# The gate projection in four pieces inside the first steps of the grid attention, and the decays by one fp32r product per head with their subtraction on ScalarE

## The reference, cut to what matters

```python
def hybrid_layer(x, ctx, ...):                      # x, ctx: 256 tokens each
    h  = modulate(rms_norm_2(x, norm1_w), sh1, sc1)
    hc = modulate(rms_norm_2(ctx, norm1_w), sh1c, sc1c)
    p  = h @ w_in                                   # q, k, v (512 each), z (512), xs, B, C, dt
    attn = neighbourhood_attention(q, k, v, kc, vc, rpb, rows)
    xs, bm, cm, dt = ssd_prep(...)                  # depthwise conv, silu, softplus
    y_ssd = ssd_bidirectional(z, xs, bm, cm, dt, a, ssd_d, ssd_norm_w, h_fwd, h_bwd)
    x = x + g1 * (concatenate([attn, y_ssd]) @ w_out)
    x = x + g2 * conv_glu(...)

def neighbourhood_attention(...):                   # per head: 256 grid keys and 256 context keys
    scores = concatenate([s_loc * scale + bias, s_ctx * scale])
    p = softmax(scores)                             # then p_loc @ v_win + p_ctx @ v_ctx

def ssd_chunked(xs, dt, a, bm, cm, h0):             # per direction
    cum = cumsum(dt * a)
    decay = exp(where(lower, cum[:, None] - cum[None, :], -inf))
    m = einsum("ign,jgn->ijg", cc, bc) * decay * dtc
    y_diag = einsum("ijge,jgep->igep", m, xc)
    y_off  = einsum(..., cc, h_in, exp(cum))

def ssd_bidirectional(z, ...):
    y = y_f + flip(y_b) + d_skip[:, None] * xs
    y = y.reshape(bsz, l, SSD_WIDTH) * silu(z)
    return rms_norm_2(y, norm_w)
```

## Time and profile before

| | |
|---|---|
| median of three executions | 1012.58 us |
| the profiled execution | 1013.08 us, its span 1011.2 us |
| TensorE busy | 978.2 us, 97% of the span |
| VectorE, ScalarE, GpSimd busy | 696.0, 511.3, 55.2 us |
| granted TensorE clock | 0.999 on the mean, the higher of its two levels (2.4 GHz) |
| grid stage, first S to first product of `w_out` | 718.7 to 783.3 us of the span |
| in it: TensorE, VectorE, ScalarE busy | 60.43, 53.49, 30.20 of 64.60 us |

### The profile page before, as it was taken

One profiled execution on the slowest core, in us unless ns is written; L12 is line 12 of the kernel. 1 busy time (PEld: TensorE's weight loads), 2 busy tenths in 40 slices (PEclk: granted clock), 3 DMA queues, 4 the chain that ended last, 5 costly groups with the idle time before them and its releaser, 6 DMA issues. The chain is left out here.

```text
span 1011.2 us, 14855 instructions
## 1 busy us (share of the span) xinstructions
PE 978.2 (97%) x5836; PEld 836.7 (83%) x5836; DVE 696.0 (69%) x997; ACT 511.3 (51%) x686; POOL 55.2 (5%) x73
## 2 busy tenths in 40 slices
PE   7989999999999999999999999999998989999997
PEld 4568899988978877899998987888865779999996
DVE  2576658999755665657778565456688587777775
ACT  2465565445446655544445563554444354444443
POOL 0210000000001200000001010000010000000000
PEclk9999999999999999999999999999999999999999
DMA  9122566767756633668887552234101336555541
GB/s 364 61 98 98 216 255 219 280 227 270 260 189 213 225 118 120 225 242 329 297 326 290 197 220 94 92 130 144 42 1 42 130 141 213 183 181 184 183 178 42
DMA packets 28943, 185.05 MB, mean 183 GB/s; under 512 B 3680, under 2 KB 4384, under 8 KB 9312
## 3 DMA queue, kind: packets, MB, share of 16 engines
q1 hardware_dynamic: 23472, 155.54, 42.6%
q0 software_dynamic: 4416, 28.31, 7.5%
q10 hardware_dynamic: 1008, 0.55, 0.2%
HBM read 181.76 MB, written 2.62 MB: 182 GB/s over the span
## 5 line engine op out<-in xcount | busy, mean ns | idle before, releaser
L1950 DVE TENSOR_TENSOR split<-raw,split 128x2048 fp32r<-128x2048 f32 x122 | 279.6, 2292 | 179.7 <-ACT split L1414 178.2
L1414 ACT ACTIVATE split<-raw 128x2048 fp32r<-128x2048 f32 x121 | 231.4, 1912 | 242.1 <-PE bank L710 224.9
L708 PE MATMUL bank<-acts,split 128*128 128x256 f32 (+1 forms) x960 | 278.5, 290 | 2.5 <-DVE acts L1990 1.4
L710 PE MATMUL bank<-acts,split 128*128 128x256 f32 (+1 forms) x960 | 276.7, 288 | 0.0
L709 PE MATMUL bank<-acts,split 128*128 128x256 f32 (+1 forms) x960 | 276.7, 288 | 0.0
L708 PE MATMUL bank<-split,acts 128*128 128x512 f32 (+1 forms) x544 | 211.1, 388 | 1.4 <-DVE split L1950 1.0
L709 PE MATMUL bank<-split,acts 128*128 128x512 f32 (+1 forms) x544 | 208.7, 384 | 0.0
L710 PE MATMUL bank<-split,acts 128*128 128x512 f32 (+1 forms) x544 | 208.6, 383 | 0.0
L708 PEld LDWEIGHTS bank<-acts,split 128*128 128x128 f32 x960 | 183.8, 191 | 10.0 <-issue 3.4
L709 PEld LDWEIGHTS bank<-acts,split 128*128 128x128 f32 x960 | 183.8, 191 | 3.6 <-issue 0.2
L710 PEld LDWEIGHTS bank<-acts,split 128*128 128x128 f32 x960 | 183.8, 191 | 1.9
(11 more groups left out here) (254 smaller groups left out, 1062.5 us busy)
## 6 DMA issues: line engine op xcount, KB each, us to landing
raw<-w_mlp SPq DMA_DIRECT2D x64, 1024.0 KB, 4.8
raw<-w_glu SPq DMA_DIRECT2D x22, 1024.0 KB, 4.8
bias<-w_ada POOLq DMA_DIRECT2D x14, 1024.0 KB, 6.7
raw<-w_qkv SPq DMA_DIRECT2D x12, 1024.0 KB, 5.1
arena<-w_glu_down SPq DMA_DIRECT2D x22, 512.0 KB, 3.3
work<-w_ada POOLq DMA_DIRECT2D x10, 1024.0 KB, 5.9
raw<-w_mla_o SPq DMA_DIRECT2D x4, 1024.0 KB, 5.1
raw<-w_moba_o SPq DMA_DIRECT2D x4, 1024.0 KB, 4.8
```

The costliest lines, as they stand in the source:

```text
L708: pe.matmul(out_, a[0], b[0], start=first, stop=False)
L710: return pe.matmul(out_, a[1], b[0], start=False, stop=last)
L1414: return act.activation(out_, in_, ACT.Copy)
L1950: v.tensor_tensor(split[:, c % 2, 1, 0:n], raw[:, c % 2, 0:n], split[:, c % 2, 0, 0:n].bitcast(F32), ALU.subtract).then_inc(lo_ready, 1)
```

## The change

1. The weights and products of z move behind those of k. z's 48 products are cut into four pieces of 12 (kind Z) that stand in steps 0 to 3 of the grid stage. ScalarE copies the two z units out of their banks at turns 3 and 5, and takes one Silu of both after the loop. VectorE multiplies by it after both y are summed.
2. The cumulative decays of the two directions lie on eight rows instead of sixteen, as a high part (rows 0 to 7) and a low part (rows 32 to 39), both fp32r. G is then one fp32r product of 128 x 512 with a column that has a one in either row.
3. The subtraction and the minimum of the decays leave VectorE: ScalarE computes relu(column - row) in four instructions right after it has copied the probabilities of turn i - 1, and then exp(-that), still in turn i. G h stands at the end of the step before that turn.
4. K goes into a small unit, which moves all small units behind it by one place, and it and the context keys' unit (C) stand ahead of P 0. `DECAY`, the places of F, Y and O, and the pair, segment and y banks are set anew.

```diff
-DECAY = (1, 2, 4, 5, 7, 8, 10, 11)
-SEGMENTS = [("G", 0), ("G", 1), ("K", 1), ("F", 0), ("G", 2), ("G", 3), ("F", 1), ("G", 4), ("G", 5), ("F", 2), ("G", 6),
-            ("G", 7), ("F", 3)]
-SEGMENT_STEP = {("K", 1): 1, **{("G", h): DECAY[h] - 2 for h in range(1, H)}, **{("F", n): 3 * n + 1 for n in range(4)}}
+DECAY = (0, 1, 5, 6, 8, 9, 11, 12)
+CARRIED = (3, 4, 8, 11)
...
+SEGMENT_STEP = {**{("G", h): DECAY[h] - 1 for h in range(1, H)}, **{("F", n): CARRIED[n] - 2 for n in range(4)}}
+MIXED = (4, 5, 7, 8, 10, 11, 13, 14)
+WEIGHTED = (3, 4, 6, 8, 10, 12, 14)
...
-    first = [("S", 0), ("S", 1), ("G", 0), ("S", 2)]
+    first = [("S", 0), ("S", 1), ("G", 0), ("S", 2), ("C", 1), ("K", 1)]
...
         steps.append(("P", i))
-        steps.extend(x for x in SEGMENTS if SEGMENT_STEP.get(x) == i)
         if i + 3 < 2 * H:
             steps.append(("S", i + 3))
-        if i - 1 in DECAY:
-            steps.append(("Y", DECAY.index(i - 1)))
-        if i % 2 == 0 and i:
-            steps.append(("O", i // 2 - 1))
+        if i < 4:
+            steps.append(("Z", i))
+        if i in MIXED:
+            steps.append(("Y", MIXED.index(i)))
+        if i in WEIGHTED:
+            steps.append(("O", WEIGHTED.index(i)))
+        steps.extend(x for x in SEGMENTS if SEGMENT_STEP.get(x) == i)
...
-            for name in ("v", "xs", "bc", "q", "z", "k"):
+            for name in ("v", "xs", "bc", "q", "k", "z"):
                 load_all(name)
...
-            rows_units(GC["z"], GU["z"], 4, 512, 512, both[:2], 2)
...
                 elif kind == "G":
                     segment_start(kind, i)
-                    for d in range(2):
-                        ins = pe.matmul(seg_bank[:, d * T:(d + 1) * T], repeated(ident, 8 * d + i, P),
-                                        cum_rows[:, d * T:(d + 1) * T], start=True, stop=True)
-                    ins.then_inc(seg_ready, 1)
+                    if i == 0:
+                        pe.wait_ge(cum_parts, 1)
+                    pe.matmul(seg_bank[:, :], repeated(pick[:, :], i, P), cumr[:, :], start=True, stop=True)\
+                        .then_inc(seg_ready, 1)
...
# ScalarE, turn i of its loop
-                if i - 1 in DECAY:
-                    h = DECAY.index(i - 1)
-                    act.wait_ge(seg_free, SEGMENTS.index(("G", h)) + 1)
-                    act.activation(E[h % 2], E[h % 2], ACT.Exp).then_inc(seg_exp, 1)
                 if i == 1:
                     context_keys(1)
+                    pair_empty(window_unit("K", 1), pair(nkT, 1))
+                    used(GC["k"] + 1)
+                if i == 3:
+                    gate_rows_out(0)
...
+                if i in DECAY:
+                    h = DECAY.index(i)
+                    segment_out(act, "G", h)
...
+                        ins = act.activation(E[h % 2][:, a:e], seg_bank[:, src:src + e - a], ACT.Relu, scale=-1.0,
+                                             bias=stat[:, c:c + 1])
+                    ins.then_inc(seg_free, 1)
+                    act.wait_ge(seg_free, SEGMENTS.index(("G", h)) + 1)
+                    act.activation(E[h % 2], E[h % 2], ACT.Exp, scale=-1.0).then_inc(seg_exp, 1)
                 if i in (6, 10):
                     pair_out(i // 4 - 1)
-                if i == 12:
-                    used(GC["k"] + 1)
+                if i in (4, 6):
+                    used(GC["z"] + i // 2 - 2)
+            for t in range(2):
+                gemm_gone(act, GU["z"] + t)
+            act.activation(sz, sz, ACT.Silu).then_inc(z_act, 1)
             pair_out(3)
...
# VectorE, after the cumulative decays, and turn i of its loop
+            step(v.tensor_tensor(pick[:, :], ident[:, 0:8], ident[:, 32:40], ALU.add))
+            step(v.tensor_copy(cumr[0:8, :], cum[0:8]))
+            settle()
+            v.tensor_tensor(cumr[32:40, :], cum[0:8], cumr[0:8, :].bitcast(F32), ALU.subtract).then_inc(cum_parts, 1)
...
-                if i in DECAY:
-                    decay(DECAY.index(i))
                 if i - 1 in DECAY:
                     matrix(DECAY.index(i - 1))
-                if i == 13:
+                if i == 1:
                     used(GC["k"] + 1)
-                if i == 14:
+                if i in (5, 7):
+                    used(GC["z"] + i // 2 - 2)
+                if i == 15:
                     gated_rows(0)
                 if i == 16:
                     gated_rows(1)
```

More of the change, by code:

```diff
@@ L204, in grid_order @@
     for kind, i in first + steps + [("T", 0), ("T", 1)]:
-        if kind in ("S", "P", "T"):
+        if kind in ("S", "P", "T", "K"):
             units[(kind, i)] = n
@@ L1164, in cumulative @@
                 b = sbank(u)
[L1165 to L1168, removed]
+                pe.matmul(b[0:8, 0:T], dA(0)[:, 0:8], const("upto"), start=True, stop=False)
+                pe.matmul(b[0:8, P:T], dA(1)[:, 0:8], const("upto", 0, P), start=False, stop=True)
+                pe.matmul(b[0:8, T:2 * T], dA(1)[:, 8:16], const("since"), start=True, stop=False)
+                pe.matmul(b[0:8, T:T + P], dA(0)[:, 8:16], const("since", P, P), start=False, stop=True)\
+                    .then_inc(small_ready, 1)
             def cumulative_columns():
@@ L1244, in segment_start, with gate_products @@
                 else:
-                    gemm_gone(pe, ku + 2)
+                    gemm_gone(pe, ku + 4)
+            def gate_products(t, part_):
+                u = GU["z"] + t
+                if t == 0:
+                    weights_in(GC["z"] + part_)
+                if part_ == 0:
+                    gemm_start(u)
+                w = slot(GC["z"] + part_, 4, 512)
+                for k in range(4):
+                    ins = product(gbank(u)[:, :], both[t](4 * part_ + k), tuple(p[:, k, :] for p in w),
+                                  part_ == 0 and k == 0, part_ == 1 and k == 3)
+                if part_:
+                    ins.then_inc(gemm_ready, 1)
+                elif t:
+                    ins.then_inc(down_used, 1)
             def grid_work(kind, i):
@@ L1773, in _ @@
                 small_empty(SU["xsrow"] + n, dst)
-            used(GC["z"])
-            used(GC["z"] + 1)
-            for t in range(2):
-                u = GU["z"] + t
-                gemm_out(act, u)
-                act.activation(sz[:, t, :], gbank(u)[:, :], ACT.Silu).then_inc(gemm_free[u % 4], 1)
             small_empty(SU["brow"], Bcr[:, :, :, :].rearrange("p a b c -> p (a b c)"))
@@ L2676, in gated_rows @@
                 v.tensor_tensor(yrow[:, t, :], y_banks[t][:, :], yrow[:, t, :], ALU.add).then_inc(y_free, 1)
-                v.wait_ge(y_free, t + 1)
-                step(v.tensor_tensor(yrow[:, t, :], yrow[:, t, :], sz[:, t, :], ALU.mult))
             def rows_means():
+                v.wait_ge(y_free, 2)
+                v.wait_ge(z_act, 1)
+                for t in range(2):
+                    step(v.tensor_tensor(yrow[:, t, :], yrow[:, t, :], sz[:, t, :], ALU.mult))
                 settle()
```

97 lines of the change are left out of this document (46 added, 51 removed).

## The result

The changed kernel takes 1037.97 us (median of 4 runs, 1036.30 to 1039.83), the kernel before 1012.62 in the same comparison: ratio 1.0252, 95% interval 1.0235 to 1.0268. The forecast was 1028.1 us with a range of 1019.5 to 1033.5. The direction was right, the size was not: 10 us are missing, and the time lies 4.5 us above the range. The profiled execution took 1037.91 us with a span of 1036.1 and a mean granted clock of 0.984, where before it was 0.999.

The account below looks back on a forecast made before the run. TensorE was taken to bound the grid stage, with ScalarE's late exponential making it wait: -8.6 gains + 23.7 new waits + 0.4 end = +15.5 us on the profiled 1013.08, giving a median of 1028.1 us, range 1019.5 to 1033.5.

Parts of the forecast that it names:

- The new wait: Grid stage, after each late G: S waits for ScalarE's tile exponential, 2.78 us for five heads; all new waits 23.7 us.
- P 1: Head 1: P 1 takes S 2's bank and waits for exponential 2 behind head 1's relu group, 3.2 us.
- P 6: Head 3: P 6 waits for VectorE's normalisation, behind ScalarE's group and pair copy, 4.6 us.
- O 6: Grid stage: O 6 waits for the third pair, behind the first y on VectorE, 0.8 us.
- The small waits at P 10 and behind the split: P 10 behind head 5, 0.7 us; after head 3 a split ahead of exponential 7, 0.5 us.
- The gains: TensorE in the grid stage: cheaper G, K in its own bank and idle time gone, together -8.6 us.
- G's 4.2 us: TensorE: eight G as one fp32r product each, 0.34 for 0.87 us, saving 4.2 us.
- z costs nothing: z's 48 products move from before the grid stage to steps 0 to 3, 10.9 us either way: 0 by itself.
- The end: End of grid stage: Silu and VectorE's work make the last pair's low part late for TensorE, 0.4 us lost.
- The clock falls: Rival: 1.2 GHz after head 1's and head 3's waits doubles the following steps, 8.9 us more, 1037.0; chance 0.08.

Follow-up runs that it names:

- the filled waits: Changed kernel plus 79 fp32r products that nobody reads, issued where TensorE waited: 1025.79 us, ratio to the kernel before 1.0110 to 1.0144.
- the kernel with G behind P: Changed kernel with G and F directly behind the transposes P of their step instead of at its end: 1013.29 us.
- both edits: Changed kernel with ScalarE's relu and decay-exponential group behind the next tile exponential, and G and F directly behind P: 1017.81 us.

## Why the prediction was wrong

- *The new wait*: right in mechanism, place and size. From G to S 3.56 us were worked out and 3.58 measured, the relu group 1.42 against 1.39 to the start of the next exponential (747.21 to 748.60). P 1 waited 3.08 (3.2 forecast), P 6 4.27 (4.6), O 6 0.76 (0.8). P 1 had two causes of nearly the same length: with G ahead 2.15 us stayed there, so its late G was worth only 0.9. Head 2 waited 2.64 and heads 5, 6 and 7 2.55 each (2.78); head 4 waited 0.38 at P 8 and 1.96 at S 11. The small waits at P 10 and behind the split did not come. Sum 20.8 for 23.7.
- *The gains*: -8.6 us should have left 66.9 us of TensorE's work with z; it is 65.5. G's 4.2 us measured 4.7 on their own.
- *z costs nothing*: right for the changed kernel, but not by itself. The split of its second chunk is what keeps 2.15 us at P 1 once G is early; the prediction saw it and counted it as covered. The first S is 10.17 us earlier (10.94 less 0.8 by which this execution was late well ahead of z), and VectorE's added three instructions lie in its idle time.
- *The end*: right. From the first w_out product to the end 227.93 before and 228.38 after, 0.45 for the 0.4 worked out, and it lies where it was put: the thirteenth product behind the last O starts 0.51 us after the twelfth (813.78, 814.29) where others follow at 0.23. The table load and what follows it, on ScalarE:

```profile
808.62 1.28 ACT L1871 ACT_TABLE_LOAD   x1
809.91 1.06 ACT L1871 ACTIVATE arena<-arena 128x1024 f32<-128x1024 f32 x1
```

As in the earlier trace rows, the instruction starts right behind the load. The drain of about 1.38 us that the Trainium skill states ("ScalarE: Activation LUTs", What ACT_TABLE_LOAD costs) is not there in this kernel either.

- *The step that failed*: all durations of the sum were taken at a clock of 1.00. What the runs showed in its place is a granted clock of 0.85 over the stage, down to 0.50 behind the new waits, and 12.9 us more of TensorE's work. The rival *The clock falls* had the chance 0.08. Its argument against was that the earlier trace rows keeps 1.00 at low use and that the earlier trace rows has waits up to 1.6 us. But these rows could not speak for seven waits of 2.0 to 4.3 us within 75 us; the trace before had none in this stage. I had named that gap in the evidence and then given the outcome 0.08. The Trainium skill ("TensorE: Matmul & The Clock Gate", Why this matters for your kernels) has idle gaps bring the clock down; the filled waits show that it holds here.
- The sum is: work 65.5 for 66.9 (-1.4), waits 20.8 for 23.7 (-2.9), clock +12.9, together +8.6 us against the forecast for the stage, from 90.6 to 99.2. The 65.5 is that of another order. From the kernel with filled waits it would be 84.9 less 79 x 0.23, 66.7 us, and the clock 11.7. The remaining 1.3 us of the 9.9 are 0.8 ahead of the stage and the spread of executions.
- The prediction also says that the trace before has no gap as long as 3.2 or 4.6 us. It has two, at its ends. The earlier trace rows lists only waits for another engine, and the longest of all is for a DMA:

```profile
PE bank L889 <- DMA arena<-w_mla_in: 6.8, 1, 6.8
```

  Behind it products of 128 x 384 take 0.85 us and more until about 12 us, and 0.49 later, though the row of the granted clock shows 1.00 there; whether they ran at the lower level is not shown. Behind the last matmul (1004.58) the row itself goes to 0.50, from 1009.5 to the end. So the chance of 0.08 stood against evidence that lay in the trace.
- The rival gave 1037.0 for the 1037.97 measured, and that is in part luck. It let the clock fall behind two waits, for 8.9 us. The clock was low behind six of the seven long ones, at a cost of 12.9, and the smaller waits and work took 4.3 us off again.

## What to carry to other kernels

A product that feeds a long chain on another engine belongs at the front of a step, with TensorE's independent work behind it; the wait is that chain less that work, and one line of order was worth 24.7 us here. When a change adds stalls of TensorE longer than any in the trace that one has, price the work behind them at both clock levels, and let the slower one carry a real part of the chance. Follow every reader of a moved result, and look for what else stands in the same turn (here a 1.9 us split, and a copy that the next normalisation needed), before moving it.

## What the runs showed of the hardware

In the changed kernel the granted clock went to 0.50, 1.2 GHz, behind stalls of TensorE of 1.96 to 3.08 us, and came back within one or two steps; the stall of 4.27 us began when it was already there. It did not follow the length of the last wait alone. Behind this one it stayed at 2.4 GHz, S at 1.12 us:

```profile
792.12 1.12 PE L1282 MATMUL bank<-arena 128*128 128x512 f32 x2 [2.55 <-ACT work L1836]
```

In the kernel with G behind P the stage's first long wait, 2.15 us at P 1, was followed by a P of 0.63 us; in the profiled execution with both edits a wait of 2.14 us at the same place by one of 1.09. There a wait of 1.39 us, ahead of an F whose P had waited 0.70, was enough too: that F took 2.08 us for 1.03. So waits below the 1.6 us of the earlier trace rows are not safe by themselves. Which of these comes out is left open; no run here separates it, and executions of one kernel differ in it. Matmuls that nobody reads, 0.23 us for 512 columns in fp32r, held the clock: 79 of them made the kernel 12.2 us shorter.
